# Low halves of the weights in a two-layer model: the last six of each hybrid stage move from GpSimd to VectorE

## The reference

```
h = x @ w_in                      # 2304 columns: dq, dk, dv, sq, sk, sv
# four differential heads: two softmaxes each, p0 - lam * p1, times v, then an RMS norm per head
# eight sliding-window heads with a sink logit: softmax(s with sink) times v
return concatenate([y_diff, y_swa]) @ w_out
```

## Time and profile before

| | |
|---|---|
| median of 3 runs | 1889.21 us (1889.15 to 1889.84) |
| the profiled execution, its time | 1889.26 us |
| its span in the trace | 1887.5 us |
| hybrid stage of the first layer in the trace | about 214 us to 324 us |
| attention items of the first layer, scores(0) to the last pv | 257.6 us to 299.8 us |
| hybrid stage of the second layer | about 708 us to 819 us |
| mean granted TensorE clock | 0.978 |

### The profile page before, as it was taken

The page is one execution under the profiler, slowest core; times in us unless marked ns, Lnnn a source line. Parts: engine busy times, 40 slices in busy tenths (PEclk is TensorE's granted clock), DMA queues, the critical chain, the costliest instruction groups (busy, mean ns, idle before and its releaser), DMA issues.

```text
span 1887.5 us, 24150 instructions
## 1 busy us (share of the span) xinstructions
PE 1787.5 (95%) x9722; PEld 1327.3 (70%) x9722; DVE 953.6 (51%) x1313; ACT 611.0 (32%) x750; POOL 149.4 (8%) x123
## 2 busy tenths in 40 slices
PE   6999999999999999999999678999998999999996
PEld 5888878788878888777887336855554777755553
DVE  3654767555555556768546994511113666511113
ACT  3543443443344335436434212210002344110110
POOL 1000051000000004110000340000000000000000
PEclk9999999999999999999999788999999999999998
DMA  7555532555455545064555002799998433799993
GB/s 274 186 179 198 195 118 90 200 188 191 178 201 184 194 178 201 24 239 179 190 188 185 21 0 89 286 422 421 421 422 322 162 134 123 313 421 421 422 422 127
DMA packets 59710, 420.43 MB, mean 223 GB/s; under 512 B 6737, under 2 KB 6737, under 8 KB 10225
## 3 DMA queue, kind: packets, MB, share of 16 engines
q1 hardware_dynamic: 55728, 404.78, 55.4%
q0 software_dynamic: 3904, 14.55, 2.3%
HBM read 418.25 MB, written 1.05 MB: 222 GB/s over the span
## 4 chain that ended last, share of the span: by engine, by line
PE 84%; DVE 9%; ACT 3%; issue 2%; POOL 1%; DMA 1%; DVEq 0%; POOLq 0%; ACTq 0%
PE hh L1089 12%; PE y L569 10%; PE y L571 10%; PE y L570 10%; PE hh L569 8%; PE hh L571 8%; PE hh L570 8%; PE turn L1115 6%; PE y L1128 3%; PE turn L1013 3%; ACT w_hi L1243 1%; DVE w_lo L1631 1%; DVE work L2054 1%; PE turn L685 1%; DVE work L2063 1%
## 5 line engine op out<-in xcount | busy, mean ns | idle before, releaser
L1631 DVE TENSOR_TENSOR w_lo<-raw,w_hi 128x2048 fp32r<-128x2048 f32 x181 | 410.9, 2289 | 159.2 <-ACT w_hi L1243 159.1
L1243 ACT ACTIVATE w_hi<-raw 128x2048 fp32r<-128x2048 f32 x193 | 364.6, 1912 | 64.9 <-DMA raw<-units 64.9
L569 PE MATMUL hh<-w_hi,xt_hi 128*128 128x512 f32 x704 | 279.8, 397 | 1.8 <-DVE xt_lo L1736 1.8
L571 PE MATMUL hh<-w_hi,xt_lo 128*128 128x512 f32 x704 | 275.3, 391 | 0.0
L570 PE MATMUL hh<-w_lo,xt_hi 128*128 128x512 f32 x704 | 275.2, 391 | 0.0
L569 PE MATMUL y<-w_hi,xt_hi 128*128 128x512 f32 (+1 forms) x480 | 191.7, 399 | 7.0 <-DVE xt_lo L2080 2.8
L571 PE MATMUL y<-w_hi,xt_lo 128*128 128x512 f32 (+1 forms) x480 | 186.9, 389 | 0.0
L570 PE MATMUL y<-w_lo,xt_hi 128*128 128x512 f32 (+1 forms) x480 | 186.9, 389 | 0.0
L569 PEld LDWEIGHTS hh<-w_hi,xt_hi 128*128 128x128 f32 x704 | 132.9, 189 | 30.1 <-DVE xt_lo L1736 2.9
L571 PEld LDWEIGHTS hh<-w_hi,xt_lo 128*128 128x128 f32 x704 | 132.7, 188 | 28.4
L570 PEld LDWEIGHTS hh<-w_lo,xt_hi 128*128 128x128 f32 x704 | 132.9, 189 | 26.3
(11 more groups left out here) (298 smaller groups left out, 2144.1 us busy)
## 6 DMA issues: line engine op xcount, KB each, us to landing
raw<-units SPq DMA_DIRECT2D x289, 1024.0 KB, 10.6
late<-units SPq DMA_DIRECT2D x96, 1024.0 KB, 11.3
ln_gb<-ln_g POOLq DMA_DIRECT2D x6, 512.0 KB, 4.0
ln_gb<-ln_b POOLq DMA_DIRECT2D x6, 512.0 KB, 5.6
x_rows<-x POOLq DMA_DIRECT2D x2, 512.0 KB, 10.0
work<-window_matrices POOLq DMA_DIRECT2D x1, 1024.0 KB, 11.0
ln_gb<-ln_mix_g POOLq DMA_DIRECT2D x2, 512.0 KB, 4.4
ln_gb<-ln_mix_b POOLq DMA_DIRECT2D x2, 512.0 KB, 5.3
```

Source lines behind the costliest of these rows:

```text
L569: pe.matmul(dst, left[0], right[0], start=start, stop=False)
L571: return pe.matmul(dst, left[1], right[0], start=False, stop=stop)
L1243: act.activation(hi[r][:, :], raw[r][:, :], ACT.Copy).then_inc(hi_ready, 1)
L1631: dve.tensor_tensor(lo[r][:, :], raw[r][:, :], hi[r][:, :].bitcast(F32), ALU.subtract)\
```

## The change

POOL loses `split_low`; DVE makes all 13 low halves of each hybrid stage. Those of units 7 and 8 come before the rotation of tile 3 (`split_to` with 9 in place of 7). Those of units 9, 10, 11 and 12 come one each at the end of items 3, 5, 7 and 10 of DVE's list. `leave_split` goes.

```diff
-            def split_low(first, last):
-
-                for n in range(first, last):
-                    pool.wait_ge(hi_ready, n + 1)
-                    pool.wait_ge(lo_ready, n)
-                    pool.tensor_tensor(lo[n % RAW][:, :], raw[n % RAW][:, :], hi[n % RAW][:, :].bitcast(F32), ALU.subtract)\
-                        .then_inc(lo_ready, 1)
-
...
-                start = (l * 2 + 1) * FF_UNITS + l * HYBRID_UNITS
-                split_low(start + 7, start + HYBRID_UNITS)
...
-            def leave_split(times):
...
                 for j in range(4):
-                    split_to((4, 6, 7, 7)[j])
+                    split_to((4, 6, 7, 9)[j])
                     wait_units((2, 4, 6, 7)[j])
...
                     if i in (13, 14):
                         sub_norm(i - 13)
+                    if i in (3, 5, 7, 10):
+                        split_to((10, 11, 12, HYBRID_UNITS)[(3, 5, 7, 10).index(i)])
...
-                leave_split(HYBRID_UNITS - 7)
                 split_to(HYBRID_UNITS + 2)
```

More of the change, by code:

```diff
@@ L1637, in split_to @@
                 split(base[0] + k - n[0])
-            def leave_split(times):
-                seen(hi_ready, times)
-                n[0] += times
-                dve.wait_ge(lo_ready, n[0])
             def wait_units(k):
```

## The result

The changed kernel is slower: 1905.33 us median of 4 executions (1902.50 to 1907.08) against 1889.19 (1889.15 to 1889.84); ratio 1.0083, 95% interval 1.0066 to 1.0101. The forecast was 1903.0. The profiled execution took 1902.50 us with a span of 1900.8, so its span is 13.3 us longer than that of before; the forecast had 13.7 on that basis. A second series of five executions gave 1902.79 us (1901.49 to 1907.35). Its times scatter more than those of the kernel before; experiments 1, 8 and 9 look for the cause.

The account below looks back on a forecast made before the run. TensorE, busy 95%, bounds most of the kernel, but in the attention ring VectorE and TensorE wait for each other. Four halves less gaps, 7.46 + 6.38, less 2 x 0.08, make 13.7 us: 1903.0 us, range 1897 to 1908.

Parts of the forecast that it names:

- The halves of units 7 and 8 cost nothing: Before the rotation of tile 3: pair hidden by tile 4 on TensorE, 0.75 and 1.2 us to spare, cost 0.
- GpSimd's halves gone: 0.08 us a layer: Combinations of items 0 and 1: first gain goes into the wait for tile 4, half of 0.16 us counted.
- Four halves at 2.24 us less the gap: Attention, ends of items 3, 5, 7, 10: first layer 8.96 less 1.50 us of idle time, 7.46 us.
- the 7 to 8 that the prediction gave as its sign: Profile sign of being right: first layer's attention longer by 7 to 8 us, the second's by 6 to 7.
- the rule: Attention ring: an inserted half costs its 2.24 us less VectorE's idle time right behind it.
- The second layer cheaper, because of its own fall of the clock: Second attention: TensorE's clock at 0.50 leaves VectorE idle 2.58 us, so four halves cost 6.38 us.
- The sum: Whole kernel: 7.46 + 6.38 - 2 x 0.08 = 13.7 us slower, 1903.0 us.
- its own account: VectorE's idle time right behind each half is all that hides it: 1900.5 to 1905 us, chance 0.63.
- Rival A: Attention: TensorE sets the pace, halves vanish in VectorE's gaps, freed port gains 3.9 us, 1885.3 us; chance 0.03.
- B: Attention: VectorE's gaps hide nearly all they can, 1897 to 1900 us, still slower; chance 0.14.
- D: First pair, before tile 3's rotation, not hidden: tile 4 and last rows wait, 1 us a layer, 1905; chance 0.05.
- Rival C: Attention: TensorE's clock falls behind the waits, at most 1 us a layer expected, 1905; chance beyond 1905 0.12.

Follow-up runs that it names:

- experiment 1: The changed kernel run once more, unaltered, for a second profile and the spread of its times: 1902.79 us median (1901.49 to 1907.35), ratio 1.0072.
- experiment 8: Changed kernel plus ten transposes nothing reads on TensorE, in front of the transposes of items 1, 3, 5 and 7: 1904.93 us, ratio 1.0082.
- experiment 9: As experiment 8, plus seven unread transposes in front of the value product of item 13: 1901.83 us, ratio 1.0071.
- experiment 5: Against the kernel with all in the gaps, unit 12's half moved to the end of item 3: 1892.54 us, ratio 1.0017.
- experiment 6: Against the kernel with all in the gaps, unit 12's half moved to the end of item 10: 1895.67 us, ratio 1.0034.
- the kernel with all in the gaps: Changed kernel with all six halves on VectorE in its long gaps, five before the attention, unit 12's behind item 0's combination: 1889.53 us, ratio 1.0004.
- experiment 2: Changed kernel with the pair of units 7 and 8 left on GpSimd, the four attention halves on VectorE: 1903.11 us, ratio 1.0079.

## Why the prediction was right

- **The halves of units 7 and 8 cost nothing.** Right, and shown by the part of the stage ahead of the attention, 53.24 to 53.26 us with the pair on either engine. VectorE kept 2.71 us in hand.
- **GpSimd's halves gone: 0.08 us a layer.** Right in kind, under-sized. Item 0's combination went to 0.48 us and into the wait for tile 4 as said. Item 3's maxima came 0.15 us closer to the first copy of tile 4 (2.96 us, against 3.11), so the whole 0.16 us was on the ring.
- **Four halves at 2.24 us less the gap.** The term that carries the result. On the chain each took 2.20, not 2.24. Counted from the first copy of tile 4, the first layer's maxima of items 4, 6, 8 and 11 are late by 1.69, 3.42, 4.52 and 6.71 us; the sum on record had 1.95, 3.90, 5.22 and 7.46 before the port's gain. The first three gaps were under-sized by 0.1 to 0.2 us each, mostly since an operation of VectorE can begin some 0.08 us before the end recorded for the one in front, which a row's idle time leaves out (the combination at 268.22 is recorded with 0.48 us, the half behind it begins at 268.62). That is the step that was off, by 0.7 us in 7.4, and the stretch of 6.72 us stayed below the 7 to 8 that the prediction gave as its sign. Experiments 5 and 6 confirm the rule at both ends: 1.69 us where there is a gap, 2.20 where there is none.
- **The second layer cheaper, because of its own fall of the clock.** Right in cause: 5.88 against 6.30 on record, just below the 6 to 7 of the sign. But the sum took off VectorE's idle time before items 4, 5, 7 and 8, and the gaps before items 5 and 7 (1.02 of the 2.58 us) don't lie right behind a half. By the rule itself it would have been 7.4 us. The maxima of item 11 come 5.89 us later (25.95 us from the first copy of tile 4, against 20.06 before). Those gaps were the cost of the half clock, 1.0 us, and in the changed kernel slower matmuls lay largely under the halves; so these gaps were hidden here although no half stands right in front of them. The fall isn't a property of that layer, though. In the kernel with all in the gaps it was in the first layer (34.31 at 0.95) and not in the second, and cost the same 1.0 us.
- **The sum.** 13.7 forecast, 13.3 in the profiled execution: 6.7 and 5.9 in the attentions, 0.8 in the state-space stage, where the length changes from profile to profile in kernels of all kinds (157.8 to 159.3 us), and a tenth or two less elsewhere. The attentions alone are 1.1 us under the forecast, so the match to 0.4 us is partly luck. The median of the first series, 1905.33, lies 0.3 us above the stretch of 1900.5 to 1905 that the prediction gave its own account, that of the second, 1902.79, inside it.
- **Rival A** (TensorE sets the pace) would have made experiments 5 and 6 free. **B** would have made the half at item 10 cheap; it cost all of 2.20 us. **D** fell with experiment 2.
- **Rival C** (the clock) is where the prediction said too little. I priced it at up to 1 us a layer among items 3 to 7. In four of the six profiled attentions with halves behind items 3, 5, 7 and 10 and no added transposes it was covered there, by the next half, to within 0.2 us; in the other two (the first of experiment 1, the second of experiment 2) a fall behind item 5 cost 1.3 and 1.5 us. What I did not see was the wait in front of the product of item 13: 0.80 us before, 0.89 after, and in the changed kernel preceded by others of 0.84 and 0.41 that the half at item 10 made. Behind it the clock fell in some executions and cost 1.2 to 2.3 us behind the attention. Three of the nine timed executions of the changed kernel are above 1905; only one of these, 1907.35, was profiled, and it has both kinds of fall.

## What to carry to other kernels

An engine that is half idle over the kernel can have no time at all in one ring of it. Before adding work there, ask of each insertion point how long the engine is idle right behind it: the operation costs its duration less that gap, once for each place. At full clock the gaps elsewhere in the ring hid about 0.1 us each here; gaps that a fall of TensorE's clock had made were hidden as well. Look first for the long idle times just ahead of the ring and at its start; here all six operations fitted into them and cost nothing. And moving work off a slow engine may only matter for what shares a port with it: check when the slow operations end against when the ring begins.

## What I had not expected

- A half on GpSimd lengthened an operation of 0.48 us with two SBUF inputs to 3.63 us, up to GpSimd's own end, while the maxima beside it, with their one tensor input in PSUM, kept their time. Under five microseconds of lateness on an engine nobody waits for cost 8.9 us, in executions in which the clock fell as well.
- TensorE waited 1.92 us and ran at half clock behind it without any loss (40.06 against 40.04 us), since the slower matmuls lay under VectorE's next half. The same fall behind a wait of 0.89 us, in front of dense matmuls, cost 1.2 to 2.3 us, and one behind a wait of 1.93 us two items later 1.3 us: where the clock falls matters more than how long the wait was.
